# VectorE makes the low parts of the weights in three stages, 24 modulation blocks move to later stages, and expert-up holds its activations stationary

## The reference

```python
mod = jnp.dot(c_act, ada_w[l]) + ada_b[l]
sh1, sc1, g1, sh2, sc2, g2 = jnp.split(mod, N_MOD, axis=-1)
...
f = jax.nn.silu(jnp.einsum('bsd,df->bsf', h, w_gate[l])) * jnp.einsum('bsd,df->bsf', h, w_up[l])
x = x + g2[:, None, :] * jnp.einsum('bsf,fd->bsd', f, w_down[l])
```

## Time and profile before

| | us |
|---|---|
| median of 3 runs (1574.42 to 1576.95) | 1575.69 |
| the profiled execution | 1575.14 |
| its span | 1573.4 |
| TensorE busy | 1442.9 |
| GpSimd busy | 1196.7 |
| VectorE busy | 957.3 |
| ScalarE busy | 811.8 |

### The profile page before, as it was taken

How to read it: one execution, slowest core, us unless ns; L and a number is a source line. 1 busy time by engine, 2 the same in 40 slices (tenths; PEclk the granted TensorE clock), 3 DMA queues, 4 the chain that set the end, 5 groups by cost and what they waited for, 6 DMA issues and landing times.

```text
span 1573.4 us, 35592 instructions
## 1 busy us (share of the span) xinstructions
PE 1442.9 (92%) x11262; PEld 1392.1 (88%) x11262; DVE 957.3 (61%) x1823; ACT 811.8 (52%) x1563; POOL 1196.7 (76%) x883
## 2 busy tenths in 40 slices
PE   1879977899989799879999999999999999999997
PEld 1659976899989688679999999999999999999997
DVE  6897859445561572741799937877774444444444
ACT  2525853454443555444688764444434555555554
POOL 1679766699999386267799986666667889899885
PEclk8799988899999899899999999999999999999999
DMA  8658655477785154144555554443434555555552
GB/s 324 225 186 318 249 201 202 146 243 251 255 293 199 67 174 167 42 134 148 164 183 182 183 180 136 136 145 134 146 133 159 177 184 185 178 184 183 180 184 94
DMA packets 77958, 285.35 MB, mean 181 GB/s; under 512 B 8784, under 2 KB 8912, under 8 KB 77392
## 3 DMA queue, kind: packets, MB, share of 16 engines
q1 hardware_dynamic: 77904, 284.63, 53.1%
HBM read 283.55 MB, written 1.05 MB: 181 GB/s over the span
## 4 chain that ended last, share of the span: by engine, by line
PE 38%; issue 20%; PEld 19%; POOL 17%; DVE 4%; ACT 1%; PEldq 1%; POOLq 0%; DVEq 0%; ACTq 0%
POOL w_lo L490 17%; PE psA L1461 12%; PE psA L1464 12%; PE psA L1465 12%; PEld psA L1465 5%; PEld psA L1464 4%; PEld psA L1461 4%; PEld psD L1807 3%; DVE arena L862 1%; PE psD L1461 1%; PEld psD L1461 1%; PEld psD L1465 1%; PE psA L1474 1%; PEld psD L1464 1%; PE psD L1464 1%
## 5 line engine op out<-in xcount | busy, mean ns | idle before, releaser
L490 POOL TENSOR_TENSOR w_lo<-raw,w_hi 128x512 fp32r<-128x512 f32 x872 | 1194.6, 1383 | 358.5 <-ACT w_hi L523 318.2
L523 ACT CAST w_hi<-raw 128x512 fp32r<-128x512 f32 x872 | 535.4, 621 | 624.5 <-PE psA L1461 422.0
L1461 PE MATMUL psA<-h_hi,w_hi 128*128 128x256 f32 x1584 | 463.1, 292 | 17.2 <-POOL w_lo L490 8.5
L1464 PE MATMUL psA<-h_lo,w_hi 128*128 128x256 f32 x1584 | 449.9, 284 | 0.0
L1465 PE MATMUL psA<-h_hi,w_lo 128*128 128x256 f32 x1584 | 449.9, 284 | 0.0
L1461 PEld LDWEIGHTS psA<-h_hi,w_hi 128*128 128x128 f32 x1584 | 305.0, 193 | 26.2 <-POOL w_lo L490 12.0
L1464 PEld LDWEIGHTS psA<-h_lo,w_hi 128*128 128x128 f32 x1584 | 305.9, 193 | 0.0
L1465 PEld LDWEIGHTS psA<-h_hi,w_lo 128*128 128x128 f32 x1584 | 305.3, 193 | 0.0
L1461 PE MATMUL psA<-u_hi,w_hi 128*128 128x256 f32 x1024 | 289.9, 283 | 2.8 <-DVE u_lo L906 2.8
L1464 PE MATMUL psA<-u_lo,w_hi 128*128 128x256 f32 x1024 | 289.8, 283 | 0.0
L1465 PE MATMUL psA<-u_hi,w_lo 128*128 128x256 f32 x1024 | 289.8, 283 | 0.0
(11 more groups left out here) (275 smaller groups left out, 1925.8 us busy)
## 6 DMA issues: line engine op xcount, KB each, us to landing
raw<-expert_down SPq DMA_DIRECT2D x128, 512.0 KB, 3.2
raw<-expert_up SPq DMA_DIRECT2D x128, 512.0 KB, 3.5
arena<-ada SPq DMA_DIRECT2D x96, 512.0 KB, 4.5
raw<-gateup SPq DMA_DIRECT2D x44, 512.0 KB, 3.3
raw<-feat SPq DMA_DIRECT2D x28, 512.0 KB, 3.8
raw<-win SPq DMA_DIRECT2D x24, 512.0 KB, 3.2
raw<-down SPq DMA_DIRECT2D x22, 512.0 KB, 3.6
raw<-wout SPq DMA_DIRECT2D x20, 512.0 KB, 3.2
```

Source lines behind the costliest of these rows:

```text
L490: nc.gpsimd.tensor_tensor(w_lo[:, s * HALF:(s + 1) * HALF], raw[:, n % 8 * HALF:(n % 8 + 1) * HALF], w_hi[:, s * HALF:(s + 1) * HALF].bitc ...
L523: nc.scalar.copy(w_hi[:, n % SLOTS * HALF:(n % SLOTS + 1) * HALF], raw[:, n % 8 * HALF:(n % 8 + 1) * HALF]).then_inc(hi_ready, 1)
L1461: first = mm(o, w[0], m[0], start=start, stop=False, skip_group_check=True)
L1464: mm(o, w[0], m[1], start=False, stop=False, skip_group_check=True)
```

## The change

VectorE makes `w_lo` for the units 61 to 126 (gate/up and down, `lower_weights` between its other steps, two units ahead) and for the 128 units of expert-up; GpSimd skips these. The modulation blocks are put in another order and other places: four of the first block (36 to 39) between the attention scores, loaded beside feat 8 to 11; none in the mLSTM loops, proj and wout; 30 in gate/up, 18 in down, eight beside query. Expert-up takes `u` stationary (two groups of 128 tokens) and 512 columns of weight moving, so that its output has tokens on partitions: ScalarE and VectorE copy it out of PSUM, TensorE turns it in 16 transposes into psD, and VectorE adds it to xT from there.

```diff
-            for j in range(3):
+            for j in range(4):
                 load(tok[j])
...
-            load(tok[3])
             stream(lambda u: tok[u + 4], 12, lambda u: ada[u + 16])
             stream(lambda u: feat[u], 8, lambda u: ada[u + 28])
-            stream(lambda u: feat[u + 8], 4)
-            stream(lambda u: feat[u + 12], 16, lambda u: ada2[u])
-            stream(lambda u: proj[u], 8, lambda u: ada[u + 36])
-            stream(lambda u: wout[u], 4, lambda u: ada[u + 44])
-            stream(lambda u: wout[u + 4], 4)
+            stream(lambda u: feat[u + 8], 4, lambda u: ada[u + 36])
+            stream(lambda u: feat[u + 12], 16)
+            stream(lambda u: proj[u], 8)
+            stream(lambda u: wout[u], 8)
...
-            with repeat(sp, 5, {units: 8, adas: 4}) as i:
+            for i in range(5):
                 for j in range(8):
                     load(gateup[i * 8 + (j + 4)])
                     if j % 2 == 1:
-                        load_ada(ada2[i * 4 + (j // 2 + 16)])
-            stream(lambda u: down[u], 12, lambda u: ada2[u + 36])
-            stream(lambda u: down[u + 12], 10)
+                        load_ada(ada2[i * 4 + j // 2])
+                    if j % 4 == 3:
+                        load_ada(ada2[i * 2 + (j // 4 + 20)])
+            stream(lambda u: down[u], 8, lambda u: ada[u + 40])
+            stream(lambda u: down[u + 8], 8, lambda u: ada2[u + 30])
+            for j in range(6):
+                load(down[16 + j])
+                if j < 2:
+                    load_ada(ada2[38 + j])
...
-            stream(lambda u: query[u], 16)
+            for u in range(16):
+                load(query[u])
+                if u % 2 == 1:
+                    load_ada(ada2[u // 2 + 40])
...
+            for first, n in ((0, DVE_FIRST), (DVE_LAST, UNITS - DVE_LOWERS - DVE_LAST)):
+                halves.n = 2 * first
+                if first:
+
+                    pool.wait_ge(lo_ready, halves.n)
+                lower_weights(n % 4)
+                with repeat(pool, n // 4, {halves: 8}):
+                    lower_weights(4)
...
-            root(xT[:, :, :], U[:, 0:KC, :], D, lambda k: (a_drained, A_AT["expert_up"] + k + 1))
+            for h in range(2):
+                act.wait_ge(sem("y_banks"), 2 * h + 1)
+                nc.scalar.copy(y_tok[:, 0, h * HALF:(h + 1) * HALF], psA[:, 2 * h, :]).then_inc(sem("y_first"), 1)
+            root(xT[:, :, :], U[:, 0:KC, :], D, lambda k: (sem("x_final"), k + 1))
...
+            def lower_weights(n_units=1):
+
+                for _ in range(2 * n_units):
+                    n = lows.n
+                    lows.n += 1
+
+                    dve.wait_ge(hi_ready, lows.value())
+                    w = slice(n % SLOTS * HALF, (n % SLOTS + 1) * HALF)
+                    V.tensor_tensor(w_lo[:, w], raw[:, n % 8 * HALF:(n % 8 + 1) * HALF], w_hi[:, w].bitcast(F32),
+                                    ALU.subtract).then_inc(lo_ready, 1)
...
                 if h % 2 == 1:
-                    ada_block(1, h // 2)
+                    ada_block(0, h // 2 + 36)
...
-                ada_block(1, h + 4)
...
-                ada_block(1, h + 8)
...
-                ada_block(1, h + 12)
...
-                ada_block(0, j + 36)
...
-                if j < 4:
-                    ada_block(0, j + 44)
...
                 Dr.free(residual(j, Dr.bank()[:, 0:T], mods[:, 0, 2 * KC:3 * KC]), settle=True)
+                if j == KC - 2:
+                    lows.n = 2 * DVE_FIRST
+                    dve.wait_ge(lo_ready, lows.n)
+                    lower_weights()
+            lower_weights()
...
-            up_chunk(0, False)
-            up_chunk(1)
-            with repeat(dve, 5, {Dr.count: 4, ada_n: 4}) as i:
-                for j in range(4):
-                    ada_block(1, i * 4 + (j + 16))
-                    up_chunk(i * 4 + (j + 2))
+            for j in range(FC):
+                lower_weights()
+                if 2 <= j:
+                    ada_block(1, j - 2)
+                lower_weights()
+                up_chunk(j, j > 0)
+                if j >= 2 and j % 2 == 1:
+                    ada_block(1, j // 2 + 19)
             f_lower(FC - 1)
...
-            for j in range(36, 48):
-                ada_block(1, j)
-            ada_bias(1, 0, 6, "ada_b2", 96)
+            for j in range(20):
+                if j < 18:
+                    ada_block(*((0, j + 40) if j < 8 else (1, j + 22)))
+                lower_weights()
+            ada_bias(0, 5, 6, "ada_b", 78)
+            ada_bias(1, 0, 5, "ada_b2", 88)
...
+            for j in range(2):
+                lower_weights()
+                u_lower(j, j, j + 1)
+            with repeat(dve, (P - 4) // 4, {lows: 8}) as i:
                 for j in range(4):
-                    u_lower(i * 4 + j, j, i * 4 + (j + 1))
-
-            dve.wait_ge(a_drained, A_AT["expert_up"])
+                    lower_weights()
+                    u_lower(i * 4 + (j + 2), (j + 2) % 4, i * 4 + (j + 3))
...
+            for h in range(2):
+                dve.wait_ge(sem("y_banks"), 2 * h + 2)
+                V.tensor_copy(y_tok[:, 1, h * HALF:(h + 1) * HALF], psA[:, 2 * h + 1, :]).then_inc(sem("y_second"), 1)
             for k in range(BANKS):
-                dve.wait_ge(a_ready, A_AT["expert_up"] + k + 1)
-                b = psA[:, (A_AT["expert_up"] + k) % BANKS, :]
+                dve.wait_ge(sem("y_turned"), k + 1)
+                b = psD[:, k, :]
...
                 pe.wait_ge(sem("u_lo"), n)
-                s = j % 4
-                row_unit(banks, (u_hi[:, s, :], u_lo[:, s, :]), first, last, A)
+                u = (u_hi[:, j % 4, :], u_lo[:, j % 4, :])
+                for h in range(2):
+                    w = half()
+                    for t in range(NT):
+                        done = product(psA[:, 2 * h + t, :], [part_[:, t * P:(t + 1) * P] for part_ in u], w,
+                                       start=first, stop=last, opens=t == 0)
+                        if last:
+                            done.then_inc(sem("y_banks"), 1)
...
+            for k in range(BANKS):
+                pe.wait_ge(sem("y_first"), k // 2 + 1)
+                pe.wait_ge(sem("y_second"), k // 2 + 1)
+                for n in range(2 * NT):
+                    j, t = 2 * k + n // NT, n % NT
+                    last = nc.tensor.transpose(psD[:, k, n * P:(n + 1) * P], y_tok[:, t, j * P:(j + 1) * P],
+                                               ident[:, :])
+                last.then_inc(sem("y_turned"), 1)
```

More of the change, by code:

```diff
@@ L67 @@
           ("ssqf", 1), ("ssq_mix", 1), ("win2_z", 8), ("ssd_decay", 20), ("ssq_ssd", 1), ("ssq_ffn", 1), ("query", 16),
-          ("experts", 128), ("expert_up", 4), ("ssq_final", 1))
+          ("experts", 128), ("ssq_final", 1))
 RING_D = (("gates", 1), ("tok", 8), ("qk", 8), ("gate_cols", 1), ("attn_scores", 8), ("m_decay", 4), ("m_scores", 4),
@@ L72 @@
 BANKS = 4
+DVE_LOWERS = 128
+DVE_FIRST = 61
+DVE_LAST = 127
 GROUP = 4
@@ L262, in two_mixers_program @@
         assert taken[0] <= 32768
+        y_tok = part(arena, 2 * KC * T, NT, D)
         nd = part(arena, ADA_SLOTS * D + 2 * D, NT * MH, MD + 1)
@@ L482, in _, with lower_weights @@
             halves = Count()
-            with repeat(pool, UNITS // 4, {halves: 8}):
-                for _ in range(8):
+            def lower_weights(n_units):
+                for _ in range(2 * n_units):
                     n = halves.n
@@ L864, in ada_block @@
                                        accum_out=mods[:, which, bass.ds(j, 1)]).then_inc(ada_used, 1)
+            lows = Count()
+            def lower_weights(n_units=1):
+                for _ in range(2 * n_units):
+                    n = lows.n
[4 more added lines that the diff above has]
+                                    ALU.subtract).then_inc(lo_ready, 1)
             def ada_bias(which, lo, hi, bias, blocks):
@@ L1138, in _ @@
             for j in range(KC):
-                if j < 4:
-                    ada_block(0, j + 44)
                 if j == 4:
-                    ada_bias(0, 3, 6, "ada_b", 64)
+                    ada_bias(0, 3, 5, "ada_b", 40)
                     gains(0, 1, 4, "norm2")
                 Dr.free(residual(j, Dr.bank()[:, 0:T], mods[:, 0, 2 * KC:3 * KC]), settle=True)
+                if j == KC - 2:
[3 more added lines that the diff above has]
+            lower_weights()
             norm_modulated("ssq2", xn, scale_cols[:, 1, :], mods[:, 0, 3 * KC:4 * KC])
@@ L1288, in _ @@
                         settle=j == 2 * QH - 1)
+                if j % 2 == 0:
+                    ada_block(1, j // 2 + 40)
+            ada_bias(1, 5, 6, "ada_b2", 96)
             own(V.tensor_tensor_scan(iota_k, ones[:, :], mask_ts[:, 0:P], -1.0, ALU.add, ALU.max))
@@ L1413, in _ @@
             multiply_late(P - 1)
+            lows.n = 2 * (UNITS - DVE_LOWERS)
+            dve.wait_ge(lo_ready, lows.n)
             def u_lower(j, slot, n):
```

(27 more changed lines are left out.)

1 line of the change is left out of this document (removed).

## The result

The changed kernel takes 1525.23 us (median of four runs, 1524.45 to 1525.37), the kernel before 1575.24 us beside it: a ratio of 0.968, 95% interval 0.9663 to 0.9697. The span of the profiled execution went from 1573.4 to 1522.9 us.

A forecast was written before the change was run, and what follows sets the result against it. TensorE was taken to bound expert-up, GpSimd to set the pace of gate/up and early down. -20.6 + 0.7 + 2.7 - 7.7 - 6.5 + 0.4 - 7 - 13 = -51.0 from 1575.14 gave 1524 us, range 1507 to 1541.

The forecast's parts named there:

- proj: Proj without its modulation blocks: 31.6 us becomes about 25.6, -6.
- wout: Wout, with VectorE close behind proj: 31.4 us becomes 24.4, -7.
- Expert-up: Expert-up with stationary activations: 512-column steps at 0.2267 us, 348.2 us instead of 368.8, -20.6.
- 0.34 at each half: Rival: each half in expert-up begins with a slow step of 0.34 us, kernel 1553 us; chance 0.07.
- 0.213 per step: Rival: the weight load's overhead hides behind the longer matmul, expert-up 327.6 us and kernel 1503; chance 0.06.
- Start of expert-up: Start of expert-up: its first two lows move to VectorE behind its last multiply, +0.7 us.
- Tail: After expert-up's last matmul: a copy and transposes come before the residuals, +2.7 us, between +2 and +4.
- Gate/up and down: VectorE makes the low parts, TensorE's 2.88 us a unit holds: gate/up -7.7, down -6.5, seam +0.4.
- that reserve: Down: -7.1 us by pace, taken as -6.5 since 16 units load a block beside each unit.
- Moved blocks: Modulation blocks taken out of mixers, proj and wout: -7 us in the mixers, -13 in proj and wout.
- the mixers: Mixers without 12 blocks: statistics start earlier, the 5.0 us wait and low clock go; -7 us, bounds -4 and -9.
- The slower rival: Gate/up and down: modulation blocks wait for DMA ahead of the lows, passing 1575 us at 1.3 us late each; chance 0.04.

The follow-up runs named there:

- experiment 2: The changed kernel, but GpSimd makes the low parts of expert-up, in its new form: 1548.9 us, ratio to the kernel before 0.984.
- Experiment 3: The changed kernel, but GpSimd makes the low parts of gate/up and down again, blocks staying moved: 1551.54 us, ratio to the kernel before 0.9856.
- experiment 4: The changed kernel with all 24 moved modulation blocks back (mixers 12, proj 8, wout 4) and the old order of transfers: 1544.82 us.
- experiment 5: The changed kernel with only the mixers' 12 modulation blocks in their old places: 1529.65 us, ratio to the kernel before 0.9717.
- experiment 7: The changed kernel plus unused matmuls of ones in TensorE's pauses, six ahead of down and ten ahead of expert-up: 1522.43 us, ratio to before 0.9668.
- experiment 1: The changed kernel with expert-up in its old form (weights stationary, 256 columns), VectorE still making its low parts: 1543.03 us, ratio to before 0.9799.
- experiment 9: The changed kernel with the first four loads of feat asked for ahead of modulation blocks 28 to 31: 1522.84 us, ratio to before 0.9674.

## Why the prediction was right

- **The sum.** -51.0 was forecast and the span fell by 50.5 (the medians by 50.0), with no term off by more than 2.7 us. That the sum came within half a microsecond is luck: expert-up gained 2.7 too little, and proj (1.2), the start (0.9, for which no term stood) and the row ahead of expert-up (0.7) made up for it, less 0.6 in wout. The terms of gate/up, down and expert-up were stages bound by one pace, 2.88 us a unit or 0.227 us a step, and both paces had been read where nothing disturbed them. Those of the moved blocks were read from waits and clocks.
- **Expert-up** is the term of largest error: -20.6 against -17.9. The step was right (0.227 in 1012 of the steps, 0.226 in 507). What was missing is the low clock at the start: twelve steps at 0.427, 12 x 0.2 = 2.4 us. The ones gave it back (348.05, the forecast 348.2). The rivals with 0.34 at each half and with 0.213 per step fell. The rule of the Trainium skill, page TensorE: Matmul & The Clock Gate, section "Back-to-back issue gap", 216 ns for 512 columns, does not hold here. That section gives it for an isolated matmul, which the prediction does not say, and 131 ns for a stream in which each matmul loads weights; the 227 ns of this stream follow neither. The term needed GpSimd silent: experiment 2 brings it back and loses 24 us, not through its own pace but through `u_lo`, which the prediction had rightly put at 0.38 for a silent GpSimd (0.42 measured).
- **Start of expert-up**: +0.44 (3.47 us of pause against 3.03), forecast +0.7. **Tail**: +2.65, forecast +2.7.
- **Gate/up and down**: -7.4 and -6.4, for the reason given: GpSimd's subtraction set the pace and VectorE's order holds no stall. Down lost 1.5 us of its pace to the low clock of its first unit (4.44 us instead of 2.9). I had taken 0.6 off for load on DMA there; every unit behind the first took 2.88, so that reserve was wrong and happened to stand for something else. That down came within 0.1 is luck too. Experiment 3 shows the cover at 26 us.
- **Moved blocks**: -20.5 with the forecast -20, and +19.6 by the medians when they are put back (+21.5 in the three stretches of that profile). For the mixers the size was right; the reason named both the block's work and its wait, and experiments 4 and 5 show that both count, without a clean split. Proj gained 1.2 more than I took, wout 0.6 less. The slower rival, late blocks in front of the low parts, did not appear: no wait for a block in gate/up or down.

## What to carry to other kernels

A stage's pace is to be read where nothing disturbs it, as time for each unit and not as busy share; and the busiest engine is not for that the one waited for: compare for each tile when it was ready with when it was used. In experiment 2 GpSimd's 1.305 us of work in a turn of 1.46 looked like the limit, yet its halves lay ready for 1.8 us and more, and a small subtraction on VectorE, which GpSimd slowed from 0.42 to 1.20, was the last to come. Parts of a change may hold each other up: here the new form needed the low parts moved (else +6 us in its stage), and so did the moved blocks (else +13). And in a queue that one engine issues in order, a load that waits for its place holds all behind it: ask of each such wait which engine must finish first, and put the loads that are needed sooner ahead of it.

## What the runs showed that was not expected

- Pauses of TensorE of 2.4 and 3.5 us can cost more than their length: up to 2.4 us behind one at the lower of the two clock levels (512 columns at 0.427 us, not 0.227). Ahead of expert-up, ten profiles without ones, with pauses of 2.83 to 3.62 us, gave clocks from 0.54 to 1.00 for the first 6 us; keeping TensorE busy with unused matmuls gave 1.00 in all three kernels that had them. Ahead of down, 2.40 us without ones gave 0.72 or 1.00. What decides within that spread stays open.
- A step of 512 moving columns takes 0.2265 us and one of 256 takes 0.120 in gate/up and expert-up: over 2.4 GHz that is 13 ns more for either, as a cost of each matmul would be.
- Down is not so steady: at granted clock 1.00 its units took 2.88 us in some profiles (the kernel before, the first of the changed kernel, experiment 7) and 2.81 in others (the second of the changed kernel, experiments 1, 2, 4 and 9), 1.5 us over the stage. So down's total of 63.31 with ones equals that of the changed kernel's second profile, which had the low clock. No run here explains it.
